# Moving the tensors of x to other offsets in SBUF, in a four-layer block stack on one core

## The reference

```python
h = rmsnorm(x, norm_mix_pre[l]); proj = h @ w_in[l]            # 1024 -> 7168 columns
...                                                            # retention, short and long convolution
merged = gates[:, :, 0] * y_ret + gates[:, :, 1] * y_sc + gates[:, :, 2] * y_cf
x = x + rmsnorm(merged @ w_o[l], norm_mix_post[l])
h = rmsnorm(x, norm_ffn_pre[l])
up = causal_dwconv(h @ w_up[l], ffn_conv_w[l]); gate, val = jnp.split(up, 2, axis=-1)
x = x + rmsnorm((jax.nn.silu(gate) * val) @ w_down[l], norm_ffn_post[l])
```

## Time and profile before

| | us |
|---|---|
| three timed runs | 2066.06, 2068.7, 2080.34 (median 2068.7) |
| the profiled execution, its own time | 2075.0 |
| its span, from the first to the last instruction | 2073.3 |

### The profile page before, as it was taken

How to read it: one execution, slowest core, us unless ns; L and a number is a source line. 1 busy time by engine, 2 the same in 40 slices (tenths; PEclk the granted TensorE clock), 3 DMA queues, 4 the chain that set the end, 5 groups by cost and what they waited for, 6 DMA issues and landing times.

```text
span 2073.3 us, 37591 instructions
## 1 busy us (share of the span) xinstructions
PE 1956.7 (94%) x15126; PEld 1853.3 (89%) x15126; DVE 1387.2 (67%) x2486; ACT 1072.1 (52%) x1812; POOL 252.4 (12%) x276
## 2 busy tenths in 40 slices
PE   8999999999899999999988889999999898899999
PEld 7889999999899899988877778999988777689999
DVE  6887888768796898667555546655575555466553
ACT  5345656645355566546644544544465535445442
POOL 1012410011014300022010002000020110030000
PEclk9999999999999999999999889999999998999999
DMA  7445545545445365634333224555443332234553
GB/s 257 159 143 174 180 146 191 196 143 188 142 157 188 120 208 193 203 134 153 125 109 105 92 72 143 183 184 190 161 148 128 120 113 89 74 126 167 185 186 110
DMA packets 86285, 315.41 MB, mean 152 GB/s; under 512 B 9568, under 2 KB 9952, under 8 KB 85984
## 3 DMA queue, kind: packets, MB, share of 16 engines
q1 hardware_dynamic: 86112, 313.01, 45.5%
HBM read 311.92 MB, written 1.05 MB: 151 GB/s over the span
## 4 chain that ended last, share of the span: by engine, by line
PE 84%; ACT 7%; DVE 5%; issue 2%; POOL 1%; DMA 1%; SPq 0%; ACTq 0%; DVEq 0%; POOLq 0%
PE big L538 73%; PE small L538 9%; ACT H L1756 3%; PE small L537 2%; PE small L541 1%; DVE POOL L1531 1%; DVE POOL L1140 1%; DMA F<-in_stream 1%; DVE L L1067 1%; POOL HL L2300 0%; ACT L1749 0%; DVE X L1132 0%; DVE POOL L1355 0%; DVE POOL L1124 0%; ACT gates L1832 0%
## 5 line engine op out<-in xcount | busy, mean ns | idle before, releaser
L1756 ACT ACTIVATE H<-F 128x1024 fp32r<-128x1024 f32 x588 | 620.4, 1059 | 833.8 <-PE big L538 829.6
L538 PE MATMUL big<-HH,H 128*128 128x256 f32 x3392 | 975.6, 288 | 6.1 <-ACT POOL L1799 1.8
L538 PE MATMUL big<-HL,H 128*128 128x256 f32 x3392 | 958.2, 282 | 4.4 <-DVE HL L1170 2.3
L538 PE MATMUL big<-HH,L 128*128 128x256 f32 x3392 | 955.2, 282 | 0.0
L1067 DVE TENSOR_TENSOR L<-F,H 128x1024 fp32r<-128x1024 f32 x588 | 722.9, 1236 | 292.3 <-ACT H L1756 291.6
L538 PEld LDWEIGHTS big<-HH,H 128*128 128x128 f32 x3392 | 650.5, 192 | 24.3 <-issue 11.2
L538 PEld LDWEIGHTS big<-HL,H 128*128 128x128 f32 x3392 | 650.6, 192 | 10.2 <-DVE HL L1170 6.3
L538 PEld LDWEIGHTS big<-HH,L 128*128 128x128 f32 x3392 | 653.0, 193 | 0.0
L538 PE MATMUL big<-FH,H 128*128 128x256 f32 x848 | 244.1, 288 | 0.0
L538 PE MATMUL big<-FL,H 128*128 128x256 f32 x848 | 240.9, 284 | 0.2
L538 PE MATMUL big<-FH,L 128*128 128x256 f32 x848 | 240.3, 283 | 0.0
(11 more groups left out here) (225 smaller groups left out, 1884.5 us busy)
## 6 DMA issues: line engine op xcount, KB each, us to landing
F<-in_stream SPq DMA_DIRECT2D x588, 512.0 KB, 3.4
X<-in_x SPq DMA_DIRECT2D x2, 512.0 KB, 4.0
out_x<-X SPq DMA_DIRECT2D x1, 1024.0 KB, 3.9
POOL<-in_decay SPq DMA_DIRECT2D x1, 768.0 KB, 9.7
CO<-in_consts SPq DMA_DIRECT2D x1, 720.0 KB, 8.3
PR<-in_params SPq DMA_DIRECT2D x1, 405.0 KB, 7.1
CO<-in_turn SPq DMA_DIRECT2D x1, 256.0 KB, 3.1
POOL<-in_lam SPq DMA_DIRECT2D x2, 128.0 KB, 4.4
```

The costliest lines, as they stand in the source:

```text
L538: return pe.e.matmul(out_, lhsT, rhs, start=start, stop=stop)
L1756: a.activation(H[:, j % NR, :], F[:, j % NF, :], ACT.Copy).then_inc(s_hi, 1)
```

## The change

Three lines of the allocation change, and a tensor that is never used is added:

```diff
@@ -276,14 +276,15 @@
         H = sb("H", [P, NR, PB * P], F32R)
         L = sb("L", [P, NR, PB * P], F32R)
         X = sb("X", [P, KT, T])
-        sb("apart", [P, 48])
+        sb("apart", [P, 32])
         HH = sb("HH", [P, KT, T], F32R)
         HL = sb("HL", [P, KT, T], F32R)
+        sb("apart2", [P, 48])
         FHa = sb("FH", [P, 14, T], F32R)
         FLa = sb("FL", [P, 14, T], F32R)
         PR = sb("PR", [P, pn])
         CO = sb("CO", [P, cn])
-        SCR = sb("SCR", [P, 240])
+        SCR = sb("SCR", [P, 264])
         POOL = sb("POOL", [P, NPOOL * T])
```

## The result

The change makes the kernel slower. Its four runs take 2,099.7 to 2,112.3 us, median 2,109.4, against 2,066.1 to 2,081.1, median 2,074.5, for the kernel before beside them: a ratio of 1.016, with a 95% interval of 1.011 to 1.022. The profiled execution took 2,109.3 us (span 2,107.6, clock 0.965). I had forecast no change, 2,069 us, with a range up to 2,105: the forecast was wrong.

What follows compares the result with a forecast made beforehand. TensorE's stream of matmuls, by the spacing of their starts, was taken to bound the kernel. All terms summed to 0 against the profiled 2,075.0 us, 6 us above the median, giving 2,069 us; range 2,036 to 2,105.

Steps and rivals of the forecast that it cites:

- I take d = 0: All 13,488 moved matmuls: the new distances change the time per matmul by 0 ns; each ns would be 13.5 us.
- The odd pairs at distance 0: Single matmuls at 52.20 and 63.63 with distance 0: next start 0.12 and 0.23 us later, like their neighbours.
- the half clock: Matmuls at 1.2 GHz: hardly any stall left at distance 192, taken as a cost of full speed whatever the distance.
- two paces with nothing else different: Long up-projection pieces: 113.5 and 118.0 ns per matmul at one distance, read as speaking against distance.
- the load of the earlier trace: Twelve matmuls with one moving column: 104 to 116 ns per load, leaving little below the quick 113.5 ns.
- 127 ns: Upper bound per 256-column matmul, 11 ns above the mean; +148 us on all 13,488 matmuls.
- The stall of the x-stationary products: Products with x stationary, distance 64: 512 columns start 0.233 us apart against 213 ns, so 20 ns lost.
- The seven pieces of the earlier trace: Chain pieces without waits: 3,702 quick and 3,294 slow matmuls, giving a mean of 115.6 ns.
- (4): x-stationary products, 288 matmuls from 64 to 128 and 24 to 192: under 0.3 us per ns, nothing.
- (5): POOL, CO, PR, SCR and gates moved for other engines: 2 us either way at most, means within 12 ns.
- The slow pace everywhere: Rival for all moved matmuls: 53% of 13,488 lose 4.45 ns each, +32 us, 2,101 us; chance 0.12.
- The quick pace everywhere: Rival for all moved matmuls: 47% of 13,488 gain 4.45 ns each, 28 us, 2,041 us; chance 0.14.

Runs made afterwards that it cites:

- experiment 11: No new change: half-clock stretches read in the profiles of the kernels with HH at 0, 96, 128, 192 and 200; 213.3 ns per matmul in every one.
- Experiment 4: Against the kernel before, only weight rings H and L moved by 64 bytes, putting x 128 past the weights; 2,108.1 us.
- experiments 1 to 3: Against the kernel before: HH and HL alone to 128, ratio 1.014; everything moved together by 192 bytes, 1.001; FH and FL alone to 64, 1.002.
- experiment 6: Against the kernel before, pads put HH, FH and the tail at other distances; ratios 1.019 (HH at 0), 1.017 (224), 1.018 (160), 1.017 (208), 1.026 (200).
- experiment 10: Against the kernel before, only the low weights L moved, by 128 bytes, timed in six runs; median 2,058.3 us, ratio 0.988.

## Why the prediction was wrong

**What bounds the kernel** was read rightly: a stream of matmuls whose spacing lies on the chain, 13.5 us for each ns. The loss is d = +3.4 ns on HH and HL, +2.3 on FH and FL and +1.7 on the tail, 3.1 on the mean; the matmuls in direct succession make 38 us of it, the span grew by 34, and the rest of the time hardly moved.

**The step that failed is "I take d = 0".** It rested on three readings, and none of them could carry it. The odd pairs at distance 0 were single matmuls. A pace is a pattern over many: at 192 the slow one repeats after three matmuls (118, 117, 118 ns and the like), at 128 the changed kernel's repeats after five (115, 117 or 118, 122, 120, 119 ns: 118.7 on the mean). One pair at 114 to 120 ns fits any of them. That distances 192 and 64 both had some stall said nothing of its size. And the half clock only shows that the stall needs the full speed, not that it is the same at every distance there: by experiment 11 all distances are alike at half clock, those that lie up to 6.7 ns apart at full clock too. In its place the runs show a pace that goes with the distance, 118.7 ns for HH and HL at 128, 117.8 for FH and FL at 64 and 117.3 to 117.5 for the tail at 160, where before all three had 113.3 or 117.8.

**The sign that was misjudged: two paces with nothing else different**. I took it as an argument against a part for distance, since both came at one distance. It was a sign that something other than the work sets the spacing, in more than one rhythm. Experiment 4 shows the partner to be TensorE's loads from H and L, experiments 1 to 3 the distance to be what decides, and experiment 6 that 192 is the only one of twelve with a rhythm of 113.3. The Trainium skill, "TensorE: Matmul & The Clock Gate", Part 2, step 1, says of the two read ports that loading the next tile's weights "doesn't steal SBUF read bandwidth from the running matmul". At half clock the trace agrees: 213.3 ns at every distance. At full clock it does not: the spacing differs by up to 6.7 ns with nothing moved but one operand (113.3 at 192, 120.0 at 200), and the measurement decides. I said that I did not lean on it, and then forecast what it forecasts.

**The bounds.** From below, the load of the earlier trace rows was the right neighbour: after the first two its starts lie 111 to 112 ns apart, which I could only put at 104 to 116, and nothing faster than 113.3 was found. From above, 127 ns was too wide; the dearest pace of a long stretch is 120.0. The stall of the x-stationary products (17.5 ns on the mean before, where I read 20 from three) goes with their 512 moving columns: at distance 128 they take 232.6 ns on the mean, at 0 (experiment 6, HH at 0) 228.0, against 230.8 before, and FH at 64 never came near 127.

**Readings to correct.** The seven pieces of the earlier trace rows have 3,438 quick matmuls; my 3,702 counts one more piece of 264 that is not among them. It moves the mean by 0.1 ns. The starts at half clock are 213.3 ns apart, not 215; that is 256 columns at 1.2 GHz, so nothing is left of the stall there, and at full clock it is 6.7 or 11.1 ns. I wrote of three odd pairs and named two.

**The other terms** held in size. (4) 0.5 us. (5) VectorE's subtraction 1,239 ns against 1,236, the ten groups next in cost within 2 ns, save two that became quicker by 15 ns (L1306) and 25 ns (L1202), 2.4 us together. I had said that all means stay within 12 ns. L1306 has its 489 ns only in the changed kernel, the only one here that moves `POOL` against the other tensors; L1202 has its 457 also where H and L alone moved (experiment 4), which are no operands of it. Neither cause was looked for.

**The rivals.** "The slow pace everywhere", 2,101 us at 0.12, came nearest: FH did go to 117.8 for good, and HH to a pace of its own, 0.9 ns beyond it. It was priced from the right row and given too little. What I wrote would make the forecast wrong, a pace that the trace of before does not have, is what came. "The quick pace everywhere" is not this change, but another placement has it, and its price was near: 28 us forecast, 23 us measured between the medians of experiment 10. That its distances are 192 and 64 together was found by trying, not foreseen.

## What to carry to other kernels

If a matmul-bound trace shows the same instructions at two steady paces, the spacing is not set by the work, and something as plain as a pad of 128 bytes can move it by 1 to 3%. Read the spacing from counts in stretches without a wait, per tensor, and try the placements of stationary and moving operands, one operand at a time; judge by the pace in the trace, which a window of 600 to 900 matmuls gives to 0.2 ns, where whole times spread by more than 1%. One odd matmul is no evidence on a steady rhythm.

## What was not expected of the hardware

- For float32r matmuls of 256 columns with a load each, at full clock, the spacing depends on the distance between the operands' starts modulo 256 bytes: 113.3 to 120.0 ns. A step of 8 bytes (192 to 200) is worth 6.7 ns, and 256 bytes more change nothing.
- Several distances have two or three steady paces. In the kernel before, one is picked after a wait and held to the next, for up to 1,488 matmuls; the picks differ between executions.
- Setting one of the two weight rings 128 bytes off (distances 192 and 64) leaves only the quick pace; 64 bytes off leaves only 118.2.
- At half clock the spacing is 213.3 ns for 256 columns at every distance, so no placement tried here costs anything there.
- ScalarE's and VectorE's work on F, H and L shows no such effect: 1,059 to 1,061 ns for ScalarE's rounding and 1,236 to 1,240 for VectorE's subtraction in every kernel here.
- Why 192, and what exactly collides between TensorE's moving read and its load, stays open.
